# A streaming gated-branch encoder step: three more pairs of gate tiles by seven products, split pooling products, and the sums of weight tiles gathered in the second token block

## The reference

```
h = rmsnorm(x, g_pre);  proj = h @ w_in                  # 1024 x (12*512 + 4*1024)
out_a = (a_u * (w_s-mix of layernorm(a_v) + b_s)) * silu(a_z)
out_b = silu(layernorm(conv31(b_a * sigmoid(b_b)))) * silu(b_z)
p     = sliding means of c_x over 2, 4, 8, 16 frames, minus c_x
out_c = einsum(p, pool_w) * pool_scale * silu(c_z)       # 4 groups, 128x128 each
out_d = d_b * conv3(d_c * d_x) * silu(d_z)
gates = sigmoid(gate_logits + b_gate)
merged = sum over branches of gates[i] * (out_i @ w_branch[i])
x + rmsnorm(merged @ w_out, g_post)
```

## Time and profile before

| | |
|---|---|
| Median of three runs | 2408.67 us |
| The profiled execution, its own time | 2408.49 us |
| Span of its trace | 2406.7 us |
| TensorE busy | 2395.3 us, 12412 matmuls |
| VectorE busy | 1457.7 us |
| GpSimd busy | 568.3 us |
| ScalarE busy | 436.7 us |
| DMA moved | 624.69 MB |

### The profile page before, as it was taken

How to read it: one execution, slowest core, us unless ns; L and a number is a source line. 1 busy time by engine, 2 the same in 40 slices (tenths; PEclk the granted TensorE clock), 3 DMA queues, 4 the chain that set the end, 5 groups by cost and what they waited for, 6 DMA issues and landing times.

```text
span 2406.7 us, 32604 instructions
## 1 busy us (share of the span) xinstructions
PE 2395.3 (100%) x12412; PEld 2072.2 (86%) x12412; DVE 1457.7 (61%) x2087; ACT 436.7 (18%) x644; POOL 568.3 (24%) x305
## 2 busy tenths in 40 slices
PE   9999999999999999999999999999999999999998
PEld 7888888788888888888888888888898999999998
DVE  7776877852456557754255656674327576677643
ACT  5222222323011111121102111111210110011111
POOL 5435444454022222222112222312200000000000
PEclk9999999999999999999999999999999999999999
DMA  8868888786766778767566777766664446988884
GB/s 335 317 241 295 309 284 293 261 303 256 255 260 219 305 258 301 281 228 270 217 245 228 281 288 294 295 231 240 244 231 178 149 141 234 327 290 263 283 280 175
DMA packets 164187, 624.69 MB, mean 260 GB/s; under 512 B 14752, under 2 KB 17184, under 8 KB 118880
## 3 DMA queue, kind: packets, MB, share of 16 engines
q1 hardware_dynamic: 150608, 598.69, 69.4%
q10 hardware_dynamic: 13456, 24.36, 2.8%
HBM read 458.83 MB, written 164.16 MB: 259 GB/s over the span
## 4 chain that ended last, share of the span: by engine, by line
PE 95%; DVE 3%; issue 1%; DVEq 0%; ACT 0%; DMA 0%; POOL 0%; POOLq 0%; SPq 0%; ACTq 0%
PE acc L1685 68%; PE acc L1899 8%; PE acc L2027 6%; PE side L1824 4%; PE side L1910 3%; PE side L1899 2%; PE acc L1789 1%; PE side L1851 1%; PE side L1841 1%; PE acc L2041 0%; PE side L1710 0%; DVE sq_x L987 0%; DVE tmp L1285 0%; DVE tmp L1587 0%; DVE tmp L1271 0%
## 5 line engine op out<-in xcount | busy, mean ns | idle before, releaser
L1685 PE MATMUL acc<-h_hi,w_pair 128*128 128x512 f32 (+1 forms) x4576 | 1304.1, 370 | 0.2 <-ACT sig L727 0.2
L1685 PEld LDWEIGHTS acc<-h_hi,w_pair 128*128 128x128 f32 x4576 | 818.6, 188 | 143.0 <-issue 2.9
L1685 PE MATMUL acc<-h_lo,w_pair 128*128 128x512 f32 (+1 forms) x2288 | 800.7, 368 | 0.0
L1685 PEld LDWEIGHTS acc<-h_lo,w_pair 128*128 128x128 f32 x2288 | 415.9, 188 | 71.2 <-issue 2.9
L1028 DVE SCALAR_TENSOR_TENSOR cb<-glu,col,cb 128x512 f32<-128x512 f32 x600 | 444.4, 806 | 21.5 <-issue 14.5
L538 POOL TENSOR_TENSOR w_pair<-w_raw,w_pair 128x1024 fp32r<-128x1024 f32 x118 | 270.0, 2300 | 272.3 <-ACT w_pair L665 257.5
L1685 PE MATMUL acc<-out_hi,w_pair 128*128 128x512 f32 (+1 forms) x896 | 277.6, 378 | 1.4 <-DVE tmp L1271 1.2
L571 POOL TENSOR_TENSOR rstd<-msq,nhalf 128x5 f32<-128x5 f32 (+4 forms) x19 | 19.4, 1024 | 818.9 <-DVE msq L956 541.1
L1685 PEld LDWEIGHTS acc<-out_hi,w_pair 128*128 128x128 f32 x896 | 163.5, 188 | 33.2 <-DVE tmp L1271 2.1
L727 ACT ACTIVATE sig<-acc,col 128x512 f32<-128x512 f32 (+1 forms) x104 | 72.0, 693 | 653.2 <-PE acc L1685 651.1
L562 POOL TENSOR_TENSOR s_lo<-w_raw,s_hi 128x1024 fp32r<-128x1024 f32 x44 | 111.8, 2562 | 231.4 <-ACT s_hi L676 231.4
(11 more groups left out here) (284 smaller groups left out, 2735.3 us busy)
## 6 DMA issues: line engine op xcount, KB each, us to landing
w_pair<-split_main SPq DMA_DIRECT2D x212, 1024.0 KB, 4.9
split_main<-w_pair SPq DMA_DIRECT2D x88, 1024.0 KB, 6.5
w_raw<-in_w_main SPq DMA_DIRECT2D x132, 512.0 KB, 5.6
chunk<-s_parts SPq DMA_DIRECT2D x88, 512.0 KB, 6.0
w_pair<-split_branch SPq DMA_DIRECT2D x72, 512.0 KB, 4.0
chunk<-split_main SPq DMA_DIRECT2D x66, 512.0 KB, 5.8
s_parts<-s_hi SPq DMA_DIRECT2D x22, 1024.0 KB, 4.0
s_parts<-s_lo SPq DMA_DIRECT2D x22, 1024.0 KB, 7.0
```

What stands on the lines that cost most here:

```text
L1685: ins = pe.matmul(acc[:, s, b, 0:m], wt[slot][:, wk], mv_[:, k, t0:t0 + m], start=(k == 0 and n == 0), stop=(k == nk - 1 and n == 2))
```

## The change

The pairs of block four now also take in the last three pairs of gate tiles of G0: `SEVEN` begins with `("G0", 3)`, so there are 25 pairs. G0 keeps one iteration of the old kind in block four. The sums of all 25 pairs are made in block two, one pair in each iteration of 2 to 21 and 23 to 27. SyncE's `s_load` now stands ahead of the weight load of the fourth unit of an iteration, and the `s_store` of the same pair ahead of the third unit's load of the iteration behind it. Block three makes none. The activation sums of block four are made earlier (`t_sums` in the M section, `t_low` in the first merge of G0), and the convolution steps move between the sections: two in each half of the pooling loop instead of one, three in M instead of four, then one after each merge of the G0 pairs. The pooled values and `poolw` are split into high and low parts, and each pooling product becomes three. `mean_mat` is gone: products with `ones` take its place, and the 1/512 is applied on VectorE (`ln_centre`) or by the column `mean_wb`.

```diff
-SEVEN = [("D", 8), ("G1", 4), ("G2", 4), ("Z", 2), ("G3", 4)]
+SEVEN = [("G0", 3), ("D", 8), ("G1", 4), ("G2", 4), ("Z", 2), ("G3", 4)]
...
-SUM_AT = [4, 6, 8, 10, 12, 14, 16, 18, 20, 24, 26]
+SUM_AT = [*range(2, 22), *range(23, 28)]
...
     def s_pair(j, it):
 
-        if 0 < j < NBLK - 1:
-            for n, at_ in enumerate(SUM_AT):
-                if 0 <= it - at_ < 2:
-                    return (j - 1) * len(SUM_AT) + n, it - at_
-        return None, None
+        if j == 1 and it in SUM_AT:
+            return SUM_AT.index(it)
+        return None
...
                 def body(i):
-                    q, phase = s_pair(j, UNIT0[name] // 4 + i)
+                    q = s_pair(j, UNIT0[name] // 4 + i)
+                    q_before = s_pair(j, UNIT0[name] // 4 + i - 1)
                     for r in range(4):
                         u = u0 + i * 4 + r
-                        if phase == 0 and r == 0:
+                        if q_before is not None and r == 2:
+                            s_store(q_before)
+                        if q is not None and r == 3:
                             s_load(q)
-                        if phase == 1 and r == 2:
-                            s_store(q)
...
                     if name == "G2":
-                        if not last:
-                            s_pair_sums(q + 8)
+                        if j == 1:
+                            for it in its:
+                                s_pair_sums(SUM_AT.index(it))
                         power(TPB + 1)
                     if name == "G3" and not last:
-                        s_pair_sums(q + 9)
+                        if j == 1:
+                            for it in its[:2]:
+                                s_pair_sums(SUM_AT.index(it))
                         power(TPB + 1)
-                        s_pair_sums(q + 10)
...
-            q, phase = s_pair(j, it)
-            if phase == 0 and r == 0:
+            q = s_pair(j, it)
+            if q is not None and r == 0:
                 act.wait_ge(s_summed, q + 1)
...
-                dve.drain().then_inc(pooled_ready, 1)
+                dve.drain()
+                dve.tensor_copy(out_hi[1][:, c, 0:w], ps[:, 0:w])
+                dve.drain()
+                dve.tensor_tensor(out_lo[1][:, c, 0:w], ps[:, 0:w], f(out_hi[1])[:, c, 0:w],
+                                  ALU.subtract).then_inc(pooled_ready, 1)
...
                 for t0, m in side_pieces(j):
-                    ins = pe.matmul(side[:, k % 2, t0:t0 + m], poolw[:, c, :], pooled[c % 2][:, t0:t0 + m],
-                                    start=True, stop=True)
+                    for n, (wt, part) in enumerate([(poolw_hi, out_hi[1]), (poolw_hi, out_lo[1]), (poolw_lo, out_hi[1])]):
+                        ins = pe.matmul(side[:, k % 2, t0:t0 + m], wt[:, c, :], part[:, c, t0:t0 + m],
+                                        start=(n == 0), stop=(n == 2))
...
-            merge(0, 0, 4, conv_at=14 if last else 6)
+            if last:
+                t_sums((3, 0), (3, 1), (3, 2))
+
+                def fourth_and_lows():
+
+                    t_sums((4, 0), (4, 1))
+                    for t in (2, 3, 1, 4):
+                        t_low(t)
+                merge(0, 0, 1, after={0: fourth_and_lows})
+            else:
+                merge(0, 0, 4, conv_at=6)
...
             if last:
+                dve.drain()
+                for q in range(3):
+                    pair_sums(q)
+                    for t in range(2):
+                        conv_step(j, 15 + 2 * q + t)
+                        seven_merge(q, t)
...
-            gated(0, 0, 4)
             if last:
+                gated(0, 0, 1)
                 seven_pairs()
             else:
+                gated(0, 0, 4)
```

More of the change, by code:

```diff
@@ L202, in build @@
     part = CT * WMAX // 2 * 4
-    t_at = [raw_at, raw_at + part, raw_at + 2 * part] + [xr_at + n * part for n in range(4)] + [bs_at]
+    t_at = [raw_at, raw_at + part, xr_at, raw_at + 2 * part] + [xr_at + n * part for n in (1, 2, 3)] + [bs_at]
     t_hi, t_lo, t_sum = {}, {}, {}
@@ L316, in banks @@
     def banks(p):
[L318 removed]
+        if PAIRS[p][0] == "D" and PAIRS[p][1] % 2:
             return [side[:, n // 2, n % 2 * 512:n % 2 * 512 + HALF] for n in range(4)]
@@ L514, in body @@
                         split_load(u, r, src, n)
-                for i in range(count // 4):
+                for i in range(1 if j == NBLK - 1 and name == "G0" else count // 4):
                     body(i)
+                if j == NBLK - 1 and name == "G0":
+                    sp.wait_ge(s_stored, 32 * NPAIR)
+                    for p in range(NPAIR):
+                        load_pair(p)
         for m in (0, 1, 4, 2, 5, 3, 6, 7):
@@ L597, in _ @@
                 n = count // 4
+                its = [u0 % UPB // 4 + i for i in range(count // 4)]
+                if j == 1 and name not in ("B", "C", "G2", "G3"):
+                    for it in its:
+                        if it in SUM_AT:
+                            s_pair_sums(SUM_AT.index(it))
                 if name in ("B", "C", "O"):
@@ L612, in _ @@
                 elif j:
[L613 to L616, removed]
                     if name == "G2":
-                        if not last:
-                            s_pair_sums(q + 8)
+                        if j == 1:
+                            for it in its:
+                                s_pair_sums(SUM_AT.index(it))
                         power(TPB + 1)
                     if name == "G3" and not last:
-                        s_pair_sums(q + 9)
+                        if j == 1:
+                            for it in its[:2]:
+                                s_pair_sums(SUM_AT.index(it))
                         power(TPB + 1)
-                        s_pair_sums(q + 10)
+                        if j == 1:
+                            for it in its[2:]:
+                                if it in SUM_AT:
+                                    s_pair_sums(SUM_AT.index(it))
                 elif n == 1:
@@ L856, in body @@
                                 s_cast(j, UNIT0[name] // 4 + i, r)
-                    if last and name == "G0":
-                        t_cast(i)
+                if last:
+                    act.wait_ge(v_stored, 16)
+                    t_cast(1)
+                    act.wait_ge(cpy_used, j * 8 + 4)
+                    t_cast(2)
+                    for r in (0, 2):
+                        sigmoid(j, u0 + r, r, q0 + qg + r // 2, r // 2, acc_free[0],
+                                c1("b_gate", BRANCHES[ph] * KT + m0 + r // 2))
+                        if r == 0:
+                            t_cast(3)
+                            t_cast(4)
+                    return
                 if n > 1:
@@ L1245, in _ @@
                 result(j, 1, c)
-                if last:
-                    conv_step(j, 10 + c)
-                elif c % 2:
+                if last and c < 3:
+                    conv_step(j, 12 + c)
+                    t_sums(*[((1, 0),), ((1, 1), (1, 2)), ((2, 0), (2, 1))][c])
+                elif not last and c % 2:
                     conv_step(j, 4 + c // 2)
@@ L1772, in _ @@
                 pe.wait_ge(w_hi_done, 1)
-            pe.matmul(side[:, 1, 0:P], mean_mat[:, :], mean_mat[:, :], start=True, stop=True)
+            pe.matmul(side[:, 1, 0:P], f(ones)[:, :], f(ones)[:, :], start=True, stop=True)
         def early_unit(u):
@@ L1918, in l_job @@
                 for t0, m in side_pieces(j):
-                    ins = pe.matmul(side[:, k % 2, t0:t0 + m], mean_mat[:, :], sq_y[:, t0:t0 + m],
+                    ins = pe.matmul(side[:, k % 2, t0:t0 + m], f(ones)[:, :], sq_y[:, t0:t0 + m],
                                     start=True, stop=True)
@@ L1930, in seven_pairs @@
                     bank = banks(p)
-                    same = name != "D" and (name, q) != ("G1", 0)
+                    same = (name, q) != ("G1", 0) and (name != "D" or q == 0)
                     if p == 0:
```

150 lines of the change are left out of this document (76 added, 74 removed).

## The result

| | median, us | runs |
|---|---|---|
| before | 2408.67 | 5, 2408.51 to 2408.72 |
| changed | 2536.84 | 5, 2535.40 to 2540.85 |

The ratio is 1.0534 (95% interval 1.0523 to 1.0545): 5.3% slower, 128 us. The forecast was 2570, its range 2520 to 2625.

The account below looks back on a forecast made before the run. TensorE bounded the kernel before; now the 26.6 us round of a pair would hold it in block two. 2408.5 + 167.9 (block two) - 5.1 (block four matmuls) + 1.6 (pairs' start) - 2.6 (pooling) = 2570.3 us, range 2520 to 2625.

Parts of the forecast that it names:

- the steps of the round: One pair's load, GpSimd's four sums, ScalarE's cast, two low parts, store and its landing before the next load: 26.6 us.
- SyncE's two waits: In block two, SyncE waits for GpSimd's low part and the stores' landing, each several us, over 20 times.
- the places of TensorE's two waits: In a G round, TensorE idles for a slot behind ScalarE's cast and for the third unit's weights: 5.0 and 5.3 us.
- 19 rounds: Block two, from the first pair's load to that of iteration 21: 19 x 26.6 = 505.4 us.
- iteration 21 to 23: Block two: iteration 22 (Z) makes no pair, and layer norm's `rstd` stands behind iteration 21's pair: 36.5 us to the next load.
- 4 rounds: Block two, from the load after iteration 22 to iteration 27: 4 x 26.6 = 106.4 us.
- last load to O: End of block two: from the last pair's load to O's first unit, 15.6 us.
- start: Block two: the first pair's load goes out one unit before V, so 5.4 us is subtracted.
- a wait of 1.6: Block four's start of pairs: third product waits for the slot VectorE frees behind four low parts; 1.6 us, between 0 and 6.
- The clock: Rival: clock falls to 1.2 GHz in block two's gaps, costing 55 us in full iterations, 2625 us; chance 0.09.
- three signs of being wrong: Rounds under 22 us; granted clock clearly under 1.00 in block two; a wait over 6 us at the start of pairs.
- The other rivals: Store's landing off the round, 2443 us, with other partial covers 0.05; weight buffers cover it all, 2402.4 us, chance 0.03.

Follow-up runs that it names:

- The spread kernel: Changed kernel with its 25 pairs of sums spread again, 13 in block two and 12 in block three, one per two iterations: 2405.72 us, ratio 0.9988.
- the gathering alone: Kernel before with only its 22 pairs of sums gathered in block two, at the changed kernel's places: 2525.41 us, ratio 1.048.
- the longer: Changed kernel with one of the four sums made three times over on GpSimd: 2608.99 us, ratio 1.0829.
- the shorter round: Changed kernel with the high sums stored as soon as ScalarE has cast them, the low ones after GpSimd's low parts: 2491.79 us, ratio 1.034.

## Why the prediction was right, and where it was off

**The direction and the mechanism** held: the steps of the round, its equality with the distance of the loads, SyncE's two waits, the places of TensorE's two waits, and that nearly all of it is block two. The spread kernel and the gathering alone show the cause from both sides; the longer and the shorter round give 23 us for each us of the round. TensorE's part in a round was not as forecast. I had it idle for about 165 us in all, 5.0 and 5.3 in a G round; it idled 87, with 0.6 and 4.6 in the round above, since the rounds were shorter and its matmuls took longer.

**The size of the round** was off, 26.6 against 25.1, and with it the sum:

| term | predicted | measured |
|---|---|---|
| 19 rounds | 505.4 | 477.0 |
| iteration 21 to 23 | 36.5 | 35.1 |
| 4 rounds | 106.4 | 99.5 |
| last load to O | 15.6 | 13.3 |
| start | -5.4 | -4.9 |
| V to O of block two | 658.5 | 619.9 |

The whole came out 33.5 us under the forecast and this stretch 38.6: the start (1.3 later) and block two's O (3.9 longer) had been put at nothing, and took a part of the error back.

I had taken the parts from one round of the kernel before, with the argument that it too followed on a store. From load to GpSimd's start it had 6.45; now it is 5.1 in most rounds. The four sums had 6.39 and now take 5.4 in the quiet rounds, 5.7 to 6.9 where VectorE is busier. Beside the sums of the row VectorE was busy for 5.2 of 6.4 us, beside those of G0 now (845.5 to 850.9) for none, and the row's load went out 3.5 us behind one of branch weights. So it seems that a slower kernel's transfers and VectorE's work crowd a round less; that is argued from the traces, not shown by a run. Two rounds point to it. When ScalarE stored 1 MB (`out_y_t`) one us after the first pair's load, GpSimd could start only 9.0 us after the load. When ScalarE had just issued 2 MB of loads (`xr`) at the end of D, the stores held the next load for 8.6 us in place of 7.3, and for 11.9 in the trace of the gathering alone. The bound I had worked out from the rows' minima, 23.6, is the round that G0 settled at, 23.74; the mean of 25.1 lies midway between that bound and the one round that I had taken.

**Block four** gained 4.3 from V to O; predicted 5.1 less a wait of 1.6, and 0.7 of pooling. The wait was 1.2 in two pieces, the first at the third product, for the merge behind the four low parts, as predicted. The pooling products gained 2.1 for 2.6.

**Block three** was costed at no gain but pooling's 0.7, and gave 2.1. The gathering alone, with plain pooling products, takes 490.6 there, 1.1 less than before, so about half is the missing sums. With its sums back (the spread kernel) it takes 491.4 again.

**The clock** rival got its rule right and its price wrong. A granted clock clearly under 1.00 in block two was one of my three signs of being wrong, and it came: 0.92 from V to O, 0.59 in the three us after a pause of 4.6. The Trainium skill, "TensorE: Matmul & The Clock Gate", HAM oscillation, says that pauses for data make the next burst start slow, and the trace agrees. The matmuls of this stretch took 42 us longer for it. But the rounds did not: I had given the clock 55 us at half speed, and no part of a round shows it. In all 25 rounds the cast began within 0.14 us of the end of the sums and the store 0.03 us after the low parts, and the next load followed 7.3 to 7.6 us later in all but two, the one beside ScalarE's loads and the one over iteration 22. So TensorE held none of the other rounds; the slow units fell into time in which it would have waited. In D the first four full units after a wait took 23.65 us in place of 21.8, inside a round of 24.3. Where TensorE itself was on the path the clock did cost. In iteration 22 Z's second and third unit, behind which the next load goes out, took 12.6 us where 10.9 is usual (granted clock 0.61, then 0.82). In block two's O the first unit took some 2 us longer (0.66, then 0.83), beside a wait of 2.0 for weights held behind the last store; that is the 3.9 which the sum had at nothing. No run holds the clock up, so this price is read from the traces alone.

**The other rivals** fell: no store went out of the round, and four buffers covered less than one round.

## What to carry to other kernels

Before a side job is made denser, add up one turn of it from the load to the release of its buffers, whatever engines it runs on, and hold that against the main engine's time for the same stretch; idle shares say nothing of it. What shares an in-order queue with the main engine's loads passes the excess on to it, once for each turn. A slower clock cost nothing here where the main engine would have waited in any case, so price it only where no such wait follows. One row of the kernel before gives one size of the turn: here it was 1.5 us above the mean, and the sum of the minima 1.5 below, each worth 35 us over 23 turns.

## What the runs showed of the hardware

- Two stores of 1 MB from one queue, issued 0.4 us apart, let the next load go after 7.3 us (8.6 and 11.9 us beside 2 MB of loads that ScalarE had issued); the second alone, issued 3.9 us after the first, after 4.8 us.
- GpSimd's 128x512 sums took 1.27 to 1.29 us each in a round with VectorE quiet, and 1.27 to 1.84 us over all of the changed kernel.
- After a pause of 4.6 us TensorE's granted clock was 0.59 over the next 3 us and 0.84 over the 3 behind, and back at 1.00 then.
